# Prompt scores in two matmuls with stacked keys, and a new order of turns, fills and loads around the first and the last pair

## The reference, cut to what matters

```
h = rmsnorm(x, g_mix)
z = h @ w_in                      # columns: u (512) | q (512) | k (512) | v (512) | forget logits (8)
s = einsum('bqhd,bkhd->bhqk', q, k) * 64 ** -0.5        # 8 heads of 64
s = s + (cq[..., None] - ck[:, :, None, :])             # sums of the log forget values
s = where(causal, s, -inf)
p = softmax(s)
o = einsum('bhqk,bkhd->bqhd', p, v)
```

## Time and profile before

| | |
|---|---|
| median of 3 runs | 902.18 us (901.16 to 902.34) |
| the profiled execution's own time | 902.74 us |
| its span in the profile | 901.0 us |
| TensorE busy, share of the span | 863.4 us, 96% |
| VectorE | 520.1 us, 58% |
| ScalarE | 369.2 us, 41% |
| GpSimd | 105.3 us, 12% |
| mean granted TensorE clock | 0.989 |

### The profile page before, as it was taken

One profiled execution on the slowest core, in us unless ns is written; L12 is line 12 of the kernel. 1 busy time (PEld: TensorE's weight loads), 2 busy tenths in 40 slices (PEclk: granted clock), 3 DMA queues, 4 the chain that ended last, 5 costly groups with the idle time before them and its releaser, 6 DMA issues.

```text
span 901.0 us, 16114 instructions
## 1 busy us (share of the span) xinstructions
PE 863.4 (96%) x6155; PEld 831.8 (92%) x6155; DVE 520.1 (58%) x944; ACT 369.2 (41%) x597; POOL 105.3 (12%) x176
## 2 busy tenths in 40 slices
PE   6989999989999999999999999999999999999996
PEld 4888988978997899989999999999999999999996
DVE  2885767667665566565667555423565642455634
ACT  6575666536435553352443333211333321233314
POOL 5014566443000020000000000000000000000000
PEclk9999999979999999999999999999999999999998
DMA  6256434217327543110332322323223323232222
GB/s 206 87 174 171 119 103 110 61 36 251 98 86 273 178 117 117 48 48 25 92 95 71 93 85 78 88 75 91 72 70 93 93 70 93 71 93 70 60 81 107
DMA packets 116507, 91.22 MB, mean 101 GB/s; under 512 B 3136, under 2 KB 107798, under 8 KB 116211
## 3 DMA queue, kind: packets, MB, share of 16 engines
q1 hardware_dynamic: 111331, 73.51, 27.1%
q0 software_dynamic: 5136, 17.17, 6.4%
HBM read 81.32 MB, written 9.35 MB: 101 GB/s over the span
## 4 chain that ended last, share of the span: by engine, by line
PE 82%; DVE 8%; ACT 4%; DMA 3%; issue 3%; SPq 0%; POOL 0%; DVEq 0%; ACTq 0%
PE ps L411 61%; PE ps L2028 3%; PE ps L1901 3%; PE ps L2172 3%; PE ps L2228 2%; PE ps L2178 1%; PE ps L2257 1%; PE ps L2278 1%; PE ps L2011 1%; PE ps L1983 1%; DMA x_tok<-in_x_sample 1%; DMA kc_raw<-in_cache_fox_k 1%; DMA w_raw<-in_w_mk 1%; DVE y_tok L1862 1%; DVE w_lo L437 1%
## 5 line engine op out<-in xcount | busy, mean ns | idle before, releaser
L437 DVE TENSOR_TENSOR w_lo<-w_raw,w_hi 128x1024 fp32r<-128x1024 f32 x103 | 126.8, 1231 | 172.8 <-ACT w_hi L432 171.0
L411 PE MATMUL ps<-a_hi,w_hi 128*128 128x288 f32 x896 | 193.5, 298 | 3.0 <-DVE w_lo L437 0.9
L411 PE MATMUL ps<-a_hi,w_lo 128*128 128x288 f32 x896 | 192.4, 296 | 0.0
L411 PE MATMUL ps<-a_lo,w_hi 128*128 128x288 f32 x896 | 192.3, 296 | 0.0
L432 ACT ACTIVATE w_hi<-w_raw 128x1024 fp32r<-128x1024 f32 x109 | 115.1, 1056 | 187.9 <-PE ps L411 179.1
L411 PEld LDWEIGHTS ps<-a_hi,w_hi 128*128 128x128 f32 x896 | 144.8, 189 | 4.3 <-issue 2.2
L411 PEld LDWEIGHTS ps<-a_hi,w_lo 128*128 128x128 f32 x896 | 144.8, 189 | 0.0
L411 PEld LDWEIGHTS ps<-a_lo,w_hi 128*128 128x128 f32 x896 | 144.7, 189 | 0.0
L411 PE MATMUL ps<-b_hi,w_hi 128*128 128x288 f32 x576 | 123.9, 297 | 1.0 <-DVE b_lo L444 1.0
L411 PE MATMUL ps<-b_hi,w_lo 128*128 128x288 f32 x576 | 123.4, 296 | 0.0
L411 PE MATMUL ps<-b_lo,w_hi 128*128 128x288 f32 x576 | 123.3, 296 | 0.0
(11 more groups left out here) (374 smaller groups left out, 1386.1 us busy)
## 6 DMA issues: line engine op xcount, KB each, us to landing
w_raw<-in_w_up SPq DMA_DIRECT2D x44, 512.0 KB, 3.8
w_raw<-in_w_down SPq DMA_DIRECT2D x16, 512.0 KB, 3.8
w_raw<-in_w_in SPq DMA_DIRECT2D x15, 512.0 KB, 4.1
w_raw<-in_w_o SPq DMA_DIRECT2D x8, 512.0 KB, 3.9
w_raw<-in_w_mq SPq DMA_DIRECT2D x8, 512.0 KB, 3.8
w_raw<-in_w_mo SPq DMA_DIRECT2D x8, 512.0 KB, 3.8
w_raw<-in_w_mk SPq DMA_DIRECT2D x6, 512.0 KB, 4.1
w_raw<-in_w_down SPq DMA_DIRECT2D x8, 384.0 KB, 3.4
```

Of the source, the lines that this page charges most:

```text
L411: mm = nc.tensor.matmul(acc[:, h, 0:H], w[slot][:, c], x[:, k, h * H:h * H + H], start=(k == first and w is w_hi and x is x_hi), stop=(k = ...
L437: nc.vector.tensor_tensor(w_lo[slot][:], w_raw[slot][:], w_hi[slot][:].bitcast(F32), ALU.subtract).then_inc(weight_lo_ready, 1)
```

## The change

1. **Stacked keys.** `k_hi` and `k_lo` become `k_both`: per head a tile whose rows of that head hold the rounded keys and whose other 64 rows hold the rest of the same keys. `q_hi` has the rounded queries in both halves of the rows. One matmul then gives hi x hi + hi x lo, and a second with `q_lo` (zeros in the other rows) gives lo x hi. The sample's own keys stay three products, from `k_own`.
2. **First pair.** VectorE's scan of the sample's decays (`cum_s`) and other work moves behind `finish_k(0)`; GpSimd loads cached keys first, cached values last; TensorE does the first four units of fill ahead of the first scores; the output copy `k_new` of pair 0 comes later.
3. **Turns.** Cached keys are turned in e3 and e7, not e2 and e5. The first turn of the sample's probabilities (entry e8) comes after the step's fill, the others before it, as all did. The exponential of the sample's row comes after the output copy on ScalarE.
4. **Fill and last steps.** `UNITS` has other numbers; `LAST_FILL` begins one step earlier, in the last step with scores (s = 43). The weight of u's third part is rounded in e5, not e7, of the last pair, and its rest is made by GpSimd, no longer by VectorE.

```diff
+    KEY_TURNS = (3, 7)
...
-        if j < PAIRS and e in (2, 5):
+        if j < PAIRS and e in KEY_TURNS:
...
-        UNITS += [3, 4, 4, 1, 1, 4, 3, 3, 3, 3, 3]
+        UNITS += [3, 3, 2, 2, 3, 4, 4, 3, 2, 3, 3]
...
-    LAST_FILL = {0: [0, 1], 1: [2, 3], 2: [4, 5], 3: [6, 7]}
+    LAST_FILL = {N_ENTRIES - 1 + i: [2 * i, 2 * i + 1] for i in range(KT // 2)}
...
-        k_hi = place("k_hi", [P, 2, T], F32R)
-        k_lo = place("k_lo", [P, 2, T], F32R)
+        k_both = place("k_both", [P, 2, 2, TP], F32R)
+        k_own = place("k_own", [P, 2, 2, TS], F32R)
...
+        def early_turns(s):
+
+            return [t for t in turns_of(s) if TURNS[t][0] == "K" or TURNS[t][1] % ENTRIES != 2 * NT]
...
-            if e == 7 and j < PAIRS:
+            if j < PAIRS and e == (7 if j < PAIRS - 1 else 5):
                 return W_QK + 2 * (j + 2)
...
-            load_decay(0, 0)
-            load_decay(0, 1)
             load_cache_k(0)
+            pool.wait_ge(cum_stored, 16)
+            load_decay(0, 0)
+            load_decay(0, 1)
+            pool.wait_ge(cum_ready, 2)
+            pool.dma_start(decay_s_dram, cum_s[:]).then_inc(cum_stored_s, 16)
+            pool.wait_ge(v_free, NT + 1)
+            expand_decay(0, 1)
+            pool.wait_ge(cum_stored_s, 16)
+            load_sample(0)
             load_cache_v(0)
-            pool.wait_ge(v_free, NT + 1)
-            load_sample(0)
-            expand_decay(0, 1)
...
+                if j == PAIRS - 1:
+                    weights_low(W_U + 2)
                 cache_values_low(j)
...
+            def second_copy(b, acc, half):
+
+                c, heads = key_pieces(acc, half)
+                for h, _, other, x in heads:
+                    copy(q_hi[other, b, Q_AT[h] + c.start:Q_AT[h] + c.stop], x, QSCALE)
+
+            def keys_high(b, acc, half):
+
+                c, heads = key_pieces(acc, half)
+                for h, own, _, x in heads:
+                    ins = copy(k_both[own, b, h, c], x)
+                return copy(k_own[:, b, 0, :], acc[:, 1, TP - H:H]) if half else ins
...
+            def keys_low(b, acc, half):
+
+                c, heads = key_pieces(acc, half)
+                for h, own, other, x in heads:
+                    ins = minus(k_both[other, b, h, c], x, f32(k_both[own, b, h, c]))
+                return minus(k_own[:, b, 1, :], acc[:, 1, TP - H:H], f32(k_own[:, b, 0, :])) if half else ins
...
-                        for q, kk in ((q_hi, k_hi), (q_hi, k_lo), (q_lo, k_hi)):
-                            ins = mm(bank[:, 0:w], q[:, b, c], kk[:, b, 0:w], start=(q is q_hi and kk is k_hi), stop=(q is q_lo))
+                        for q in (q_hi, q_lo):
+                            ins = mm(bank[:, 0:w], q[:, b, c], k_both[:, b, e // NT, 0:w], start=(q is q_hi), stop=(q is q_lo))
```

More of the change, by code:

```diff
@@ L518, in half_task, with key_pieces @@
             return n, half, (n - W_QK) // 2, (n - W_QK) % 2
+        def key_pieces(acc, half):
+            w = H if half == 0 else TP - H
+            return slice(half * H, half * H + w), [(h, slice(h * DH, h * DH + DH), slice(DH - h * DH, P - h * DH), acc[h * DH:h * DH + DH, half, 0:w])
+                                                   for h in range(2)]
         def query_pieces(q, acc, half):
@@ L1040, in finish_q @@
                 copy(by_half(q_hi[0:DH, b, 0:T]), halves(acc[0:DH]), QSCALE)
+                for half in range(2):
+                    second_copy(b, acc, half)
                 for d, x in second_head(q_hi[DH:P, b], acc[DH:P]):
@@ L1062, in finish_half @@
                     c = slice(half * H, half * H + H)
[L1063 removed]
+                    keys_high(b, acc, half)
                     ins = copy(k_new[:, j, c], acc[:, half, 0:H])
@@ L1132, in _ @@
                     copy(o_aux[0:DH, 0:wide].rearrange("p (g q) -> p g q", q=q), groups_of(OB[DH:P, n % 2, 0:2 * wide], q)[:, :, 0]).then_inc(o_aux_ready, 1)
+                if s < N_ENTRIES and e == ENTRIES - 1:
+                    exponentials(s)
                 if pair_after(s) is not None:
@@ L1633, in _ @@
                     finish_u(2, 0)
+                if s == 1:
+                    rest_of_weights(dve, 7, 1)
                 n = weights_after(s)
-                if n is not None and n >= W_U + 2:
+                if n is not None and n >= W_U + 3:
                     dve.wait_ge(weight_lo_ready, n)
@@ new lines, in fill @@
+            def fill(s):
+                for u in fill_units(s):
+                    n, half, _, _ = half_task(u // KT)
+                    k = u % KT
+                    if k == 0:
+                        if half == 0:
+                            pe.wait_ge(weight_lo_ready, n + 1)
+                        if n == W_QK + 2:
+                            pe.wait_ge(acc_free, A_QK + 1)
+                        elif half == 0:
+                            pe.wait_ge(half_free, n - W_QK - 2)
+                        else:
+                            pe.wait_ge(acc_free, A_QK + n - W_QK)
+                    for w, x in ((w_hi, a_hi), (w_hi, a_lo), (w_lo, a_hi)):
+                        ins = mm(ACC[0][:, half, 0:H], w[n % 2][:, k * P:k * P + P], x[:, k, half * H:half * H + H],
+                                 start=(k == 0 and w is w_hi and x is a_hi), stop=(k == KT - 1 and w is w_lo))
+                    if k == KT - 1:
+                        ins.then_inc(weight_used if half else half_done, 1)
@@ L1967, in _ @@
             for s in range(STEPS):
                 j, e = divmod(s, ENTRIES)
+                if s == 0:
+                    fill(0)
                 if s < N_ENTRIES:
@@ L2032, in _ @@
-                if j == PAIRS and e in LAST_FILL:
-                    if e == 0:
+                for t in early_turns(s):
+                    turn_into(t)
+                if s > 0:
+                    fill(s)
+                if s in LAST_FILL:
+                    if s == N_ENTRIES - 1:
                         pe.wait_ge(weight_lo_ready, W_U + 3)
                         pe.wait_ge(acc_free, A_U + 2)
-                    project(0, a_hi, a_lo, ACC[0], LAST_FILL[e], KT)
+                    project(0, a_hi, a_lo, ACC[0], LAST_FILL[s], KT)
@@ L2037, in _ @@
+                for t in turns_of(s):
+                    if t not in early_turns(s):
+                        turn_into(t)
                 for g in values_of(s):
```

143 lines of the change are left out of this document (66 added, 77 removed).

## The result

The changed kernel is **slower**: 904.0 us median of 18 runs against 901.23 of the kernel before on the same chip, ratio of the means 1.0027 with a 95% interval of 1.0019 to 1.0035, so 2.4 us more where 5.7 less were forecast. The profiled execution took 904.20 us (902.74 before).

A forecast was written before the change was run, and what follows sets the result against it. TensorE, busy 863.4 of 901.0 us, was taken as the bound. Gains of 1.5 (A) and 5.8 (C) less 1.6 (B) made 5.7, so 902.74 became 897.0, with a range of 888 to 902.5.

The forecast's parts named there:

- e3: Step where the key turn now precedes a turn of probabilities: TensorE waits 0 to 2 us, taken as 1.0.
- e7: Step where the second key turn is now made: VectorE has `kc_lo` done 4.1 us after this step's scores.
- e8: Step where turned probabilities need the second key turn's bank: wait of 0.9, up to 1.6; 2.0 in pair 0.
- A: Stretch from the opening to the start of pair 1: 8.4 us gone, 6.9 of new waits, so 1.5 gained.
- C: Stretch from pair 3 to the projection behind the last values: 5.8 us gained, 4.5 of it from half clock.
- B: Middle stretch from pair 1 to pair 3: 2.8 us saved and 3.6 paid per pair, so 1.6 lost.
- third matmuls: Prompt's scores: 8 dropped per pair at 0.17 us each, 5.4 over four pairs if TensorE has other work.
- The rival with the clock: Clock falls in the middle pairs behind waits of 2.6 us: 910, or 903 with shorter falls; chance 0.10.
- second copies of q: ScalarE's two more pieces per half of q, 0.82 us, ahead of the exponentials: waits of 1.3 and 0.9 in A.
- e4: Step 4 of the pair in A: its values, with those of step 6, wait 0.9 us (0 to 1.6) for q's pieces.
- own keys' values: Last pair: these values lose their cover of 12 matmuls, so TensorE waits 1.7 us.
- GpSimd's queue: Middle pairs: `w_lo` is ready 9.5 us after the later key turn, so TensorE waits about 2.6 in its fill.

The follow-up runs named there:

- no_second_q: Changed kernel without ScalarE's second copies of the rounded queries in the fill, matmuls unchanged: 899.07 us, ratio 0.9970 to the kernel before.
- old_plus_last: Kernel before with the last pair's part alone (earlier fill of u's third part, its weight's rest by GpSimd): 897.94 us, ratio 0.9956.
- last_back: Changed kernel with the last pair's part undone: 902.79 us, ratio 1.0000 to the kernel before.
- no_third: Kernel before without the matmul of q_hi and k_lo in the prompt's scores, all copies kept: 901.09 us, ratio 0.9989.
- no_pieces2: Changed kernel without ScalarE's second query copies and without the second head's key pieces on ScalarE and VectorE in the fill: 897.07 us, ratio 0.9948.
- old_last_turn: Kernel before with the last pair's part and the later turn of the sample's first probabilities, keys not stacked: 894.15 us, ratio 0.9915.
- stack_plus_last: Kernel before with stacked keys, the last pair's part and the later turn of the sample's first probabilities; opening, key turns and units old: 904.90 us, ratio 1.0026.
- old_last_turn_37: old_last_turn with the changed kernel's places of key turns and its new fill units, keys not stacked: 898.43 us, ratio 0.9966.
- old_last_open: Kernel before with the last pair's part and the new opening order, keys not stacked: 897.57 us, ratio 0.9949.
- turns_back: Changed kernel with cached keys turned at their old places again, new units of fill kept: 903.3 us, ratio 1.0015 to the kernel before.
- stack_only: Kernel before with stacked keys alone; turns, units, opening and last pair old: 914.04 us, ratio 1.0140.

## Why the prediction was wrong

**The step that failed: the time at half clock.** The sum credited two stretches at half clock as gone, "the half clock behind it, 4.62 x (1 - 0.63) = 1.7" in A and "Without the 2.1 wait the half clock goes too: 9.06 x 0.50 = 4.5" in C, and put in nothing for a fall of the clock behind its own new waits. Together these 6.2 us are more than the whole gain of 5.7. In the profile both stretches are gone, but three others came: 6.8 us in A, 3.4 in B and 3.4 behind the last values. They lose 6.8 us (half of 13.6), as much as the two before. By kinds of term, in us:

| term | forecast | profile |
|---|---|---|
| TensorE's waits in the attention | +5.2 | +5.3 (17.1 for 11.8) |
| TensorE's work (third matmuls -5.2, a unit of fill +0.4) | -4.8 | -4.3 (its busy time, with as much half clock in both) |
| lost at half clock | -6.2 | 0.0 (6.8 for 6.8) |
| sum (by rounded terms to 0.2) | -5.7 | +1.2 (the span) |

The waits came as forecast in total, in part by luck, since their places differ; 6.2 of the 7.2 us by which the profiled execution missed 897.0 are the clock. (A slip of 0.4 stands beside it: the unit of fill that C is charged with leaves A, and A is not credited.) Over the runs the mean granted clock is 0.9925, against 0.990 of the kernel before in the other comparisons: by the span that would be about 2 us gained, not 6.2, and it is an upper estimate. Of the 18 runs of the changed kernel the six at 0.989 to 0.991 take 904.8 us on average and the twelve at 0.993 to 0.996 903.5, so 1.3 us where 0.0038 of the span would be 3.4.

The rival with the clock was weighed by "A wait of 2.1 was followed by 9 us of work at half clock, 4.5 lost; one of 1.4 was not", and took 2.6 as the danger. It left out the wait of 2.9 in the earlier trace rows, with half clock 1.2 us behind its end, and that several of the new waits were put between 1.4 and 2.1. Here the clock fell at 78.5, 143.3 and 204.8. The last two are 1.7 us behind the end of waits of 1.54 and 1.77 (at 141.59 and 203.08). At the first, TensorE had waited 1.29 until 77.34, worked for 0.4 and stood in a wait of 1.65 until 79.43. Waits of 1.59 (the first keys) and of 1.55, 1.47 and 1.51 (at 110.29, 124.97 and 157.38) were followed by none. The size of one wait does not decide. The Trainium skill's rule on this (TensorE: Matmul & The Clock Gate, "HAM oscillation — how this bites in real kernels"), cold starts behind waits, fits the places where it fell, and says nothing here on why the other four did not. That a wait causes the fall is not shown by an experiment of its own; that both go together is (no_second_q, old_plus_last, last_back).

**What a part is worth, first: "8 go in each pair ... four pairs 5.4, if TensorE has other work to go on to", with "that is not so everywhere" left without a price.** As TensorE's own time the price is about right, but by no_third the matmuls are worth 1.0 us. TensorE arrives earlier at a chain of score, exponential, turn and `pt` on the other engines, and in no_third it waits 1.8 us longer for it in the middle pairs. In the sum this stands among the waits, which is why the total did not fail by it; as the worth of stacking it misleads. The Trainium skill's price for one (same page, "Back-to-back issue gap"), 4.3 us for the 32 by my estimate, misses in the same way: no price of a matmul answers that question.

**Second: the pieces were priced only at the places where I saw a wait.** For the second copies of q I had 1.3 and 0.9 in A, 1.0 a pair in e3 and nothing in C, 4.2 in all; no_second_q gives 5.1. The second key pieces give 2.0 (no_pieces2), and stacking by itself costs 10 (old_last_turn against stack_plus_last). VectorE waits for a half's last copy (1.31 us in the rows of e3), so what is added on ScalarE delays both queues. In the middle pairs I summed 3.6 us of waits a pair, and 3.6 and 3.2 came (1.55 + 0.60 + 1.47 in pair 1), but from other places: no wait for GpSimd, more on VectorE.

What was right, by its steps:
- e8: 0.9 to 1.6 forecast, 1.47, 1.51 and 0.83 came in pairs 1 to 3, through the instructions that I walked; in pair 0 it did not come, a like one stood in e4 instead (1.65).
- e3: 1.0 (0 to 2) forecast, 1.55 and 1.54 came.
- own keys' values: 1.7 forecast, 1.77 came. Own and first keys: 1.3 forecast, 1.59. First scores: 1.4, now 0.77 + 1.29.
- GpSimd's queue: 9.5 us from the key turn to `w_lo` forecast; the turn ended at 120.38 and `w_lo` by the rows below at 129.77, which is 9.4. It did not bind because TensorE was late as well (fill at 129.90), behind the waits of 0.60 and 1.47 in e7 and e8. Where VectorE is early it binds: 1.6 a pair in old_last_turn_37.
- C's size, 5.8 against 5.4; but nearly all of it is the half clock (5.1; the waits changed by 0.5, 3.5 gone and 3.0 new), and a part comes back behind 203 (3.4 us at half clock, 1.7 lost).

GpSimd's queue in the changed kernel, pair 1:

```profile
121.77 2.79 POOL L837 TENSOR_TENSOR vc_both<-vc_raw,vc_both 128x256 fp32r<-128x256 f32 x4
124.52 1.55 POOL L844 TENSOR_TENSOR b_lo<-inv_rms,b_hi 128x288 fp32r<-128x288 f32 x2
126.02 0.92 POOL L871 DMA_DIRECT2D vc_raw<-in_cache_fox_v  x1
126.96 2.81 POOL L829 TENSOR_TENSOR w_lo<-w_raw,w_hi 128x256 fp32r<-128x256 f32 x4
```

The parts, in us of the kernel before:

| part | from, to | us |
|---|---|---|
| last pair's part | before, old_plus_last | -4.0 |
| later turn of the sample's first probabilities | old_plus_last, old_last_turn | -3.7 |
| opening order | old_plus_last, old_last_open | -0.6 (not measurable) |
| new places of key turns and fill | old_last_turn, old_last_turn_37 | +4.6 |
| stacked keys | old_last_turn, stack_plus_last | +10.0 |
| all (not additive) | before, after | +2.4 |

The two costs overlap: in the stacked kernel the key turns' places are worth only 1.1 (turns_back, with the new units), and from old_last_turn to the changed kernel both and the opening together cost 10.1. **Open stays** why the last part gains 4.0 in the old order and costs 2.4 in the changed kernel; the granted clock goes with it in both (0.990 to 0.993, and 0.9945 to 0.9925), by the span some 2 us each, and what decides where the clock falls was not settled.

## What to carry to other kernels

That TensorE is busy 96% of the span does not make each of its instructions worth its time. Take one out with nothing put in its place first: that run prices the gain before any work is moved to other engines. Where an engine's queue feeds a chain of short steps, each piece put ahead of it can cost its whole length, though the engine is busy only 42% of the span: twelve copies, 4.5 us of ScalarE's time, cost 5.1. A change of several parts should be measured in parts: two parts of this one gain 7.7 us together, and two others with the opening lose 10.1. Here the waits that went took their half clock along, but other falls of the clock came in other places and lost as much: time at half clock should not be credited as gained while the change makes new waits.

## What the runs showed of the hardware that was not expected

In the changed kernel the clock fell to 0.50 behind waits as short as 1.5 to 1.8 us, and did not behind others of 1.5 to 1.6. Kernels that differ by some us of waits differ in their mean granted clock as well (stack_only 0.986, the kernel before 0.990, last_back 0.9945); 0.004 of clock is 3.6 us of this span. But the clock is not paid in full: within the runs of the changed kernel 0.0038 of it went with 1.3 us.

TensorE is busy 95 to 96% of the span in both kernels, and still 4.5 us of ScalarE's copies taken out of the changed one gave 5.1 us (4.7 at like clock), while 32 matmuls (5.4 by start to start) taken out of the kernel before gave 1.0.
